# A two-block transformer on one core: eight modulation tiles and the value bias on VectorE, start-up loads and modulation reordered

## What is computed

```
def modulate(h, shift, scale):
    return h * (1.0 + scale[:, None, :]) + shift[:, None, :]
...
        ada_x = jnp.split(s_lat @ w_ada[l] + b_ada[l], 6, axis=-1)
        ada_c = jnp.split(s_ctx @ w_ada[l] + b_ada[l], 6, axis=-1)
        hc = modulate(rmsnorm(ctx, norm_mix_g[l]), ada_c[0], ada_c[1])
        pc = hc @ w_in[l][:, ML_START:MERGE_START] + b_in[l][ML_START:MERGE_START]
        _, ctx_state = mlstm_branch(pc[..., :ML_COLS], pc[..., ML_COLS:], ...)
        hx = modulate(rmsnorm(x, norm_mix_g[l]), ada_x[0], ada_x[1])
        yx, _ = token_mixer(hx, *mix_params, rows, GRID_W, ctx_state)
        x = x + ada_x[2][:, None, :] * yx
        hx2 = modulate(rmsnorm(x, norm_ffn_g[l]), ada_x[3], ada_x[4])
        x = x + ada_x[5][:, None, :] * expert_choice_ffn(hx2, w_router[l], ...)
```

## Time and profile before

| what | value |
|---|---|
| median of 3 runs | 2276.83 us (2274.57 to 2279.39) |
| the profiled execution | 2277.35 us, of which the span of the trace is 2275.5 us |
| PE busy | 1904.8 us (84%) |
| VectorE busy | 708.1 us (31%) |
| ScalarE busy | 335.3 us (15%) |
| mean granted TensorE clock | 0.923 |
| DMA | 648.59 MB |

### The profile page before, as it was taken

One profiled execution on the slowest core, in us unless ns is written; L12 is line 12 of the kernel. 1 busy time (PEld: TensorE's weight loads), 2 busy tenths in 40 slices (PEclk: granted clock), 3 DMA queues, 4 the chain that ended last, 5 costly groups with the idle time before them and its releaser, 6 DMA issues.

```text
span 2275.5 us, 30074 instructions
## 1 busy us (share of the span) xinstructions
PE 1904.8 (84%) x12730; PEld 1278.0 (56%) x12730; DVE 708.1 (31%) x1663; ACT 335.3 (15%) x759; POOL 0.2 (0%) x4
## 2 busy tenths in 40 slices
PE   7899999966666666666666679999999999999999
PEld 4688778521111111111111137868889978688899
DVE  3433334300000000000000025562556556625654
ACT  4132030200000000000000010260210012612100
POOL 0000000000000000000000000000000000000000
PEclk7999999987788888878788889999999999999999
DMA  7456578999999999999999995524644554246441
GB/s 265 167 186 215 192 248 308 398 429 428 428 429 429 428 429 428 429 429 429 429 429 429 429 401 181 183 77 167 241 149 166 187 204 166 94 167 227 162 167 56
DMA packets 147882, 648.59 MB, mean 285 GB/s; under 512 B 10645, under 2 KB 17410, under 8 KB 123016
## 3 DMA queue, kind: packets, MB, share of 16 engines
q1 hardware_dynamic: 144100, 643.81, 71.5%
q10 hardware_dynamic: 3684, 3.37, 0.5%
HBM read 646.10 MB, written 1.05 MB: 284 GB/s over the span
## 4 chain that ended last, share of the span: by engine, by line
PE 60%; DMA 33%; DVE 4%; issue 1%; ACT 1%; SPq 0%; ACTq 0%; DVEq 0%
DMA ring<-in_w_exp 33%; PE bank L2016 15%; PE bank L890 13%; PE bank L2699 6%; PE bank L1799 4%; PE bank L1551 4%; PE bank L2614 2%; PE bank L1814 2%; PE bank L904 1%; PE bank L933 1%; PE bank L931 1%; PE bank L611 1%; PE bank L768 1%; PE bank L1476 1%; PE bank L451 1%
## 5 line engine op out<-in xcount | busy, mean ns | idle before, releaser
L1799 PE MATMUL bank<-ring,arena 128*32 128x512 f32 x1968 | 301.1, 745 | 212.3 <-DMA ring<-in_w_exp 202.0
L1799 PEld LDWEIGHTS bank<-ring,arena 128*32 128x32 f32 x1968 | 60.2, 123 | 436.5 <-DMA ring<-in_w_exp 320.4
L890 PE MATMUL bank<-hx,ring 128*128 128x256 f32 x1344 | 293.2, 379 | 0.7 <-ACT hx L786 0.7
L890 PEld LDWEIGHTS bank<-hx,ring 128*128 128x128 f32 x1344 | 254.6, 190 | 37.5 <-issue 3.4
L1814 PE MATMUL bank<-ring,arena 128*32 128x512 f32 x1008 | 165.5, 799 | 77.5 <-DMA ring<-in_w_exp 66.6
L1857 DVE COPY arena<-bank 128x256 f32<-128x256 f32 x16 | 6.8, 424 | 525.8 <-PE bank L1804 525.8
L2016 PE MATMUL bank<-arena 128*128 128x256 f32 x672 | 151.0, 379 | 0.3 <-DVE arena L2065 0.3
L1814 PEld LDWEIGHTS bank<-ring,arena 128*32 128x32 f32 x1008 | 33.3, 134 | 193.8 <-DMA ring<-in_w_exp 111.2
L2016 PEld LDWEIGHTS bank<-arena 128*128 128x128 f32 x672 | 127.0, 190 | 17.5 <-DVE arena L2065 0.6
L1864 DVE COPY arena<-bank 128x256 f32<-128x256 f32 x16 | 6.8, 424 | 346.1 <-PE bank L1688 346.1
L2016 PE MATMUL bank<-ring,hx 128*128 128x256 f32 x448 | 105.8, 379 | 0.0
(11 more groups left out here) (484 smaller groups left out, 2285.9 us busy)
## 6 DMA issues: line engine op xcount, KB each, us to landing
ring<-in_w_exp SPq DMA_DIRECT2D x186, 2048.0 KB, 16.3
ring<-in_w_ada SPq DMA_DIRECT2D x36, 2048.0 KB, 12.2
ring<-in_w_in SPq DMA_DIRECT2D x29, 2048.0 KB, 9.2
ring<-in_w_ffn_in SPq DMA_DIRECT2D x20, 2048.0 KB, 8.0
ring<-in_w_ffn_out SPq DMA_DIRECT2D x10, 2048.0 KB, 7.8
ring<-in_w_out SPq DMA_DIRECT2D x6, 2048.0 KB, 10.9
arena<-in_w_exp SPq DMA_DIRECT2D x4, 2048.0 KB, 19.2
ring<-in_w_up_nsa SPq DMA_DIRECT2D x2, 2048.0 KB, 8.4
```

What stands on the lines that cost most here:

```text
L890: ins = pe.matmul(b[:, o:o + n], w[:, k, j * P:(j + 1) * P], h[:, k, :], start=k == 0, stop=k == KD - 1)
L1799: ins = pe.matmul(banks[s][32 * j:32 * j + 32, :], e_xe[:, 2 * t + kk, :], w[:, kk, 512 * j:512 * j + 512], start=t + kk == 0, stop=t + kk ...
```

## The change

1. **Start.** The three loads of the first filter layer go from ScalarE's queue to the head of SP's, the identity the other way. The sums of squares of ctx go behind the second filter layer on ScalarE. On VectorE the mean and the scale of the norm go behind all eight tap products, and the sums of the taps behind these. `act_tables` goes ahead of the copies of the turned x and ctx. The five spectra of order 0 go from ahead of the tables to between the second and third modulation tile.
2. **Modulation.** VectorE modulates x, ScalarE ctx. `dve_wide_first` replaces four T and four S steps by the order S1, T1, S2, T2 ("sums 6"), S3, T3 ("sums 7"), S4, T4; PE waits for these names in turn. `dve_gate_pad` moves behind it.
3. **Value bias.** The six bias matmuls go; VectorE adds a broadcast bias row (five additions).
4. **Later tiles 0 to 7** are multiplied on VectorE: eight chained operations of 128x512 a tile (`dve_later_sum`), placed as the diff shows, and PE sums over partitions by four matmuls a tile. Four `pe_later` calls stand in `pe_project` and four in `pe_branches`; the one behind `pe_mlstm_num(pe, 3)` is gone. The stream order follows.

```diff
@@ stream @@
-    tiles("v", wide(w_in, ML0 + 1024, ML0 + 1536))
+    tiles_and_ada("v", wide(w_in, ML0 + 1024, ML0 + 1536))
...
-        (tiles_and_ada if t < 1 else tiles)(f"hy{t}", wide(w_in, 512 * t, 512 * t + 512))
-    tiles_and_ada("o", wide(w_in, ML0 + 1536, ML0 + 2048))
+        (tiles_and_ada if t != 1 else tiles)(f"hy{t}", wide(w_in, 512 * t, 512 * t + 512))
+    tiles("o", wide(w_in, ML0 + 1536, ML0 + 2048))
...
-    tiles_and_ada("", [])
@@ def dve_filter_taps(v) @@
-        v.wait_ge(*K.loaded("load_dft"))
...
+        dve_stats_mean(v)
+        dve_stats_scale(v)
+        DV.stage("filter")
+        v.wait_ge(*K.loaded("load_dft"))
+        for o in range(2):
+            for c in range(NC):
...
@@ def pe_ada @@
-            if t == 2:
-                pe_spectra(pe, 1, (0, 1))
+            if t in ADA_FILL:
+                pe_spectra(pe, *ADA_FILL[t])
+    ADA_FILL = {1: (0, range(5)), 2: (1, (0, 1))}
@@ def pe_later(pe) @@
+            if i < ON_DVE:
+                pe.wait_ge(*at(f"later summed{i}"))
+                for j in range(4):
+                    ins = pe.matmul(banks[6][32 * j:32 * j + 32, (i % 4) * P:(i % 4 + 1) * P], ones[:, 0:32],
+                                    later_acc[i % 2][:, j * P:(j + 1) * P], start=True, stop=True)
+                ins.then_inc(*PE.step(f"full later rows{g}", f"later read{i}"))
+                continue
+    ON_DVE = 8
+    def dve_later_sum(v, i, part):
+        w = tile(v, f"later{i}")
...
+        for k in (0, 1, 2, 3) if part == 0 else (4, 5, 6, 7):
+            c = cT[:, k, 0:1]
+            if k == 0:
+                v.tensor_scalar(acc, w[:, k, :], c, None, ALU.mult).then_inc(*DV.step())
+            else:
+                v.wait_ge(*DV.last())
+                v.scalar_tensor_tensor(acc, w[:, k, :], c, acc, ALU.mult, ALU.add).then_inc(*DV.step())
@@ def pe_seven_wide @@
-                if key == "v" and bias is not None:
-                    ins = pe.matmul(o, ones[0:1, 0:P], bvrow[:, 256 * bias:256 * bias + 256], start=False, stop=True,
-                                    skip_group_check=True)
...
-        pe.wait_ge(*at("S project"))
-        pe.wait_ge(*at(f"T4 {key}"))
+        pe.wait_ge(*at("sums 6" if key == "k" else f"T2 {key}"))
...
+        if key == "k":
+            pe.wait_ge(*at("sums 7"))
@@ def dve_seven_wide @@
+                with_bias(u.rearrange("p (c n) -> p c n", c=2), nh)
+                v.wait_ge(*DV.last())
                 v.tensor_tensor((vc, vx)[th][:, :, 2 * nh:2 * nh + 2, 0:P], f(b), f(u), ALU.add).then_inc(*DV.step(*names))
+        def with_bias(x, nh):
+            v.tensor_tensor(x, x, spread(bvrow[:, 256 * nh:256 * nh + 256], 1, 2), ALU.add).then_inc(*DV.step())
@@ def dve_project(v) @@
+        dve_wide_first(v)
+        dve_gate_pad(v)
...
-        dve_seven_wide(v, "v", lambda i: None)
+        dve_seven_wide(v, "v", lambda i: dve_later_sum(v, i // 2, i % 2))
         dve_conv(v, 1)
+        for i in (2, 3):
+            dve_later_sum(v, i, 0)
+            dve_later_sum(v, i, 1)
         dve_rows(v)
         dve_conv(v, 2)
+        for i in (4, 5):
...
         dve_conv(v, 3)
         dve_context(v)
+        for i in (6, 7):
...
         dve_conv(v, 4)
@@ def act_branches(act) @@
         act.wait_ge(*at("tokc"))
+        act_later(act, 2)
+        AC.stage("mlstm")
...
-        act_later(act, 2)
```

More of the change, by code:

```diff
@@ L575, in act_ada @@
             ada_cols.append(f"full {name} col{t}")
[L576 to L577 removed]
+            if t - 1 in ADA_FILL:
+                act_spectra(act, *ADA_FILL[t - 1])
                 AC.stage("ada")
@@ L616, in pe_later @@
         PE.cur = stage
+    ON_DVE = 8
+    later_acc = [arena[:, 14368 + 512 * i:14880 + 512 * i] for i in range(2)]
+    def dve_later_sum(v, i, part):
+        w = tile(v, f"later{i}")
+        acc = later_acc[i % 2]
+        if part == 0 and i > 1:
+            v.wait_ge(*at(f"later read{i - 2}"))
+        for k in (0, 1, 2, 3) if part == 0 else (4, 5, 6, 7):
[5 more added lines that the diff above has]
+                v.scalar_tensor_tensor(acc, w[:, k, :], c, acc, ALU.mult, ALU.add).then_inc(*DV.step())
+        if part:
+            book.where[f"later summed{i}"] = DV.now
+            book.where[f"used {where[f'later{i}']}"] = DV.now
     def pe_later_turn(pe, g):
@@ L625, in act_later @@
     def act_later(act, g):
-        act.wait_ge(*at("m3 v"))
+        act.wait_ge(*at("v sums"))
         if g:
@@ L717, in act_normed, with act_modulate_c, dve_modulate_x @@
                 *AC.step(f"{key} normed"))
-    def act_modulate_x(act):
+    def act_modulate_c(act):
         AC.stage("norm")
-        act.wait_ge(*at("gain mix0"))
+        act.wait_ge(*at("gain c"))
         for k in range(KD):
-            act.activation(hcx[:, k, N:2 * N], scrx[:, k, :], ACT.Identity, bias=adaX[0][:, k:k + 1],
-                           scale=gs[:, k:k + 1]).then_inc(*AC.step("hx done"))
-    def dve_modulate_c(v):
+            act.activation(hcx[:, k, 0:N], scrc[:, k, :], ACT.Identity, bias=adaC[:, k:k + 1],
+                           scale=gsC[:, k:k + 1]).then_inc(*AC.step("hc done"))
+    def dve_modulate_x(v):
         DV.stage("norm")
-        v.wait_ge(*at("turncn in3"))
+        v.wait_ge(*at("turnxn in3"))
         for k in range(KD):
-            v.tensor_scalar(hcx[:, k, 0:N], scrc[:, k, :], gsC[:, k:k + 1], adaC[:, k:k + 1], ALU.mult, ALU.add).then_inc(
-                *DV.step("hc done"))
+            v.tensor_scalar(hcx[:, k, N:2 * N], scrx[:, k, :], gs[:, k:k + 1], adaX[0][:, k:k + 1], ALU.mult, ALU.add).then_inc(
+                *DV.step("hx done"))
     def pe_turn_in(pe, key, src):
@@ L923, in pe_seven_wide, with product @@
         S1, S2, S3, S4 = wide_s
-        def product(name, b, h, x, first=False, bias=None):
+        def product(name, b, h, x, first=False):
             for j in range(2):
@@ L969, in dve_wide_t, with dve_wide_first @@
             v.tensor_tensor(T4, quarter(w, 1, 0), T2, ALU.subtract).then_inc(*DV.step(f"T4 {key}"))
-    def dve_wide_s(v):
+    def dve_wide_first(v):
         S1, S2, S3, S4 = wide_s
+        w = tile(v, "k0")
+        T1, T2, T3, T4 = wide_t["k"]
+        v.wait_ge(*DV.last())
         v.wait_ge(*at("hc done"))
-        v.wait_ge(*at("hx done"))
         v.tensor_tensor(S1, wide_part(1, 0), wide_part(1, 1), ALU.add).then_inc(*DV.step())
-        s1 = DV.last()
-        v.tensor_tensor(S3, wide_part(0, 0), wide_part(1, 0), ALU.subtract).then_inc(*DV.step())
-        v.wait_ge(*s1)
-        v.tensor_tensor(S2, S1, wide_part(0, 0), ALU.subtract).then_inc(*DV.step())
-        v.wait_ge(*DV.last())
-        v.tensor_tensor(S4, wide_part(0, 1), S2, ALU.subtract).then_inc(*DV.step("S project"))
+        v.tensor_tensor(T1, quarter(w, 0, 1), quarter(w, 0, 0), ALU.subtract).then_inc(*DV.step())
+        v.wait_ge(*DV.last())
+        v.tensor_tensor(S2, S1, wide_part(0, 0), ALU.subtract).then_inc(*DV.step())
+        s2 = DV.last()
+        v.tensor_tensor(T2, quarter(w, 1, 1), T1, ALU.subtract).then_inc(*DV.step("sums 6"))
+        t2 = DV.last()
+        v.tensor_tensor(S3, wide_part(0, 0), wide_part(1, 0), ALU.subtract).then_inc(*DV.step())
+        v.tensor_tensor(T3, quarter(w, 1, 1), quarter(w, 0, 1), ALU.subtract).then_inc(*DV.step("sums 7"))
+        v.wait_ge(*s2)
+        v.tensor_tensor(S4, wide_part(0, 1), S2, ALU.subtract).then_inc(*DV.step())
+        v.wait_ge(*t2)
+        v.tensor_tensor(T4, quarter(w, 1, 0), T2, ALU.subtract).then_inc(*DV.step("T4 k"))
     def dve_seven_wide(v, key, after):
@@ L1012, in dve_seven_wide @@
         put(0, 1, b3, wu2, f"free {key}r3", f"{key} sums")
+        if key == "v":
+            v.wait_ge(*at("v copied"))
+            for c in range(NC):
+                x = vc[:, c, 0:2, 0:P]
+                v.tensor_tensor(x, x, bvrow[:, 0:256].rearrange("p (h e) -> p h e", h=2), ALU.add).then_inc(
+                    *DV.step("v sums"))
     def pe_project(pe):
@@ L1219, in dve_project @@
         v.wait_ge(*at("columns"))
-        for i in range(4):
-            dve_wide_t(v, "k", i)
-        dve_wide_s(v)
+        dve_wide_first(v)
+        dve_gate_pad(v)
         v.wait_ge(*at("full spec14"))
@@ L2916, in _ @@
         pe_turn_in(pe, "turncn", cin)
-        pe_spectra(pe, 0, range(5))
         pe_tables(pe)
```

57 lines of the change are left out of this document (26 added, 31 removed).

## The result

| | median us (lowest to highest, runs) | profiled run, span us |
|---|---|---|
| before | 2277.22 (2274.05 to 2279.45, 20) | 2277.35, 2275.5 |
| after | 2282.89 (2281.56 to 2284.78, 20) | 2284.72, 2282.9 |

The ratio is 1.0029, with a 95% interval of 1.0023 to 1.0035: the change makes the kernel slower by 5.7 us, a quarter of a percent. The forecast was 2276.0 and "no change that can be measured".

The account below looks back on a forecast made before the run. PE bounds until 353 us, expert weight loads from 462 to 1400. Gains of 5.7 + 4.9 + 8.8 us shrink to 1.6 through waits, less 0.7 at the branches' end: 0.9 us, median 2276.0, range 2266 to 2284.

Parts of the forecast that it names:

- the bias: Value product v: six bias matmuls and their effect on the neighbours go from PE's path, 4.9 us won.
- the modulation and the sums: k's second product starts at 72.7 instead of 77.78 and the clock stays up; PE 5.7 us ahead at product 7.
- the wait of 3.5 us ahead of the turn: After the taps PE waits 3.5 us for last tap, mean, scale and norm before turning x.
- the fourth part's price: Between v's end and the Hyena matmuls: 8.8 us of PE calls saved, but load and VectorE waits leave 1.6 us overall.
- hy0 lands at 136.4 ... 0.5 us: Behind v: hy0's load, queued behind tiles 2 and 3, lands after PE wants it at 135.9; wait 0.5 us.
- wanted at 150.9: 1.9 us: hy1's load, behind tiles 4 and 5, lands at 152.8, so PE waits 1.9 us.
- seven chained operations of 0.69 ... with 0.03 between, 5.5 us: One later tile on VectorE: a tensor_scalar of 0.47 and seven chained operations, 5.5 us in all.
- the o linear loses 1.5: Behind the wait for tiles 6 and 7 the clock is at half, costing the o linear 1.5 us.
- The rival in which the sums run at the rate of tensor_scalar: Later tiles take 3.8 us each, both VectorE waits shrink by 3.4; time 2269; chance 0.14 for VectorE half in the way.
- The end of the branches: Without the call the turn starts 0.3 us earlier, PE idles 4.1 us, the clock likely halves; 0.7 us lost.
- The start: From the first filter loads to the last modulation turn (63.2 against 64.04): the reordering earns 0.9 us.
- the clock stays low: After the pause ahead of the turn the clock rises only after the spectra, at 53: 7.3 us lost, 2283.3; chance 0.19.

Follow-up runs that it names:

- the kernel with all tiles on PE: Changed kernel with its fourth part undone (later tiles' sums, calls and stream as before; start, modulation and bias stay changed): 2264.74 us, ratio 0.9947.
- the fourth part alone: Kernel before with only the sums of tiles 0 to 7 on VectorE, their new calls, places and stream: 2293.15 us, ratio 1.0065.
- half of the sums: Changed kernel with VectorE leaving out four of the eight blocks of each of tiles 4 to 7: 2274.24 us, ratio 0.9988.
- the kernel with the last call moved: Changed kernel with the last call of later tiles (14 and 15) behind the last numerator again: 2281.94 us, ratio 1.0024.
- six summed in VectorE's idle time: Changed kernel with only tiles 0 to 5 summed on VectorE, placed around its row work: 2257.35 us, ratio 0.9917.

## Why the prediction was wrong

**What held.** The bound and that a shift before the merge arrives at the end; the bias (4.9 forecast; alone 4.9 in the trace and 4.7 by the medians); the modulation and the sums (with the start 5.7 forecast at product 7; 4.5 in the profiled pair, 5.7 in the kernel with all tiles on PE, where it begins at 80.49; the three parts together bring 10.5 us at v's end in that kernel's trace, against 5.7 + 4.9); the place and the size of the waits ahead of the state (6.4 and 6.40) and ahead of the call for tiles 6 and 7 (5 and 5.40); the wait of 3.5 us ahead of the turn; that a call fewer at the end of the branches only leaves PE idle.

**What failed: the fourth part's price.** By the prediction it costs, between v's end and the Hyena matmuls, 9.1 us (102.9 from 118.5 to 221.4, against 93.84). Measured: 15.0 in after and 15.6 where it was alone (129.06 to 238.49, less 93.84). Of the 5.9 us between forecast and after, 5.7 are these terms of the sum:
- "hy0 lands at 136.4 ... 0.5 us" and "wanted at 150.9: 1.9 us": 1.46 and 3.06, so 2.1 more. The order in the queue of loads was followed rightly, but counted from v's end hy0 was there 0.9 us and hy1 2.2 us later than reckoned.
- A term that wasn't there: the clock behind the load wait. It was counted for pauses of 5 us only. hy1 lost 1.4 in after, 1.7 in the kernel with the fourth part alone, and 3.0 with half of the sums, against its 14.08 elsewhere. So 1.4 more.
- "seven chained operations of 0.69 ... with 0.03 between, 5.5 us": 0.752 each, 0.79 from start to start, 6.0 us a tile. Tiles 4 and 5 are 1.0 of this (it shows as the wait of 1.06 ahead of tile 5's read), and from kw to the read of tile 7 it takes 11.95 us (197.18 to 209.13) instead of 11.0: 2.0 more for the four tiles.
- "the o linear loses 1.5": it lost 2.2. From the read of tile 7 to its end it takes 16.7 us instead of 16.3, and ScalarE behind it 2.9 instead of 3.1: 0.2 more.

The 0.69 came from an operation of the same name and width whose scalar is an immediate (L1412, after L1467). Here it is a column in SBUF, a value per partition. That this is the reason the other widths in the trace of after show (line, operation, form, count, busy us, mean ns of one); L840 has a column, L424 and L1467 an immediate, and all read and write SBUF:

```profile
L840 DVE SCALAR_TENSOR_TENSOR scr<-xT,small,rs 128x256 f32<-128x256 f32 x32 | 13.0, 479 | 0.1
L424 DVE SCALAR_TENSOR_TENSOR arena<-mg,arena 64x256 f32<-64x256 f32 x6 | 2.5, 418 | 0.2
L1467 DVE SCALAR_TENSOR_TENSOR arena<-arena 128x512 f32<-128x512 f32 x4 | 2.8, 692 | 10.7 <-ACT arena L1447 10.7
```

With a column it is 752 against 692 at 512 columns, 479 against 418 at 256, and 348 (L2831) against 285 (L2211) at 128: 60 to 63 ns more at each width. The trace of before had such rows too: the convolution (L1107), which the prediction used for its 4.4 us, takes 476 ns for 252 columns. The rival in which the sums run at the rate of tensor_scalar is refuted by the rows of the tiles: the first operation of each takes 0.48, the other seven don't. The table of the Trainium skill, page "VectorE: DVE Perf Modes", section "The perf-mode tier table", doesn't list the operation; 752 ns here against 481 for tensor_scalar at the same width agree with the reading that it has no double rate.

**The end of the branches** was priced at 0.7; from L1531 to the merge after takes 1.2 more than before, and the three other kernels without that call take 130.7 to 131.1 us. But with the call it takes 129.4 to 130.8 in nine traces, so a part of the 1.2 may be the clock of that one execution. With v's end at 119.9 instead of 118.5 this makes the whole miss at the merge: 5.9 + 0.5 + 1.4 = 7.8 us, against 7.9 from -0.9 to 7.0.

**The start** was forecast at +0.9. It is 1.8 when done alone, within the error of nothing, and -0.2 in the two profiled runs. In that of after the taps began at 16.52 instead of 16.1 and the turn took 6.53 us instead of the forecast 5.9. In the nine traces with the pause the turn took between 5.30 and 6.53, by how soon its transposes came to full speed. Of the rival "the clock stays low", nothing was found: it is at 1.00 from 40 us to the end of v.

**The sign** turned on a difference of two large sums, 19.4 us won and 18.5 given away, and the second held only the waits that I had found. The error of 5.9 us on it was larger than the result. A forecast of "same" at 0.57, with a rival slower by 5 us or more only through the clock at the start, left out the plainest one: that the waits and the sums are each a little longer than reckoned, and that a shorter pause too can be followed by the lower clock. The measured 2282.89 lies within the stated 2266 to 2284, but by luck: the upper part of that range was given to a clock that stays low at the start, and it did not.

## What to carry to other kernels

Moving work from the bound engine to an idle one pays only where the idle time lies in front of what the bound engine waits for. Eight tiles, four of them summed where PE waits for them, cost 16 to 18 us; six summed in VectorE's idle time won some 7. So read the idle engine's timeline against the deliveries between the two, and give a wait that the work itself brings (a later load, an eviction behind it) its own term. Price an operation by a row with the same kind of operands (here a column as the scalar), and a chained one by start-to-start distance. Give the low clock a price behind every pause of the sizes seen here, 2 to 6 us, as a chance and not only behind the longest.

## What the runs showed of the hardware

- **What the clock costs behind a pause varies from execution to execution.** A pause of about 3 us ahead of hy1 cost 1.4 us (after), 1.7 (the fourth part alone, 15.77 instead of 14.08), 3.0 (half of the sums, 17.12) and nothing in the kernel with the last call moved: there the same wait of 2.78 was followed by a linear of 14.08. The merge takes 29.55 or 27.86 us in traces of kernels with the same code there: 29.55 in before and 27.86 in the kernel with the last call moved, each behind a pause of 2.10 and the same rows ahead of it. The Trainium skill, page "TensorE: Matmul & The Clock Gate", section "HAM oscillation — how this bites in real kernels", lets each burst behind a pause pay again; these traces agree, except that not every one paid. The profiled run of after, 2284.72 us, is the second longest of its twenty, so the 7.4 us between the two traces hold 1.8 that the medians don't; that these are the clock's is likely and not shown.
- **The granted clock of a row is not the whole truth.** In the trace with all tiles on PE it reads 1.00 from 17 to 31 us, yet the taps take 13.99 us, as in before, where it reads 0.50. The length of matmuls of a known form decides.
- **scalar_tensor_tensor with a column as its scalar** takes 752 ns for 128x512, fifty-six times within 750 to 754, and with an immediate 692; the 60 ns are the same at 256 and 128 columns.
- **A chain of VectorE and ScalarE over 4 partitions** (the row work) takes 13.4 to 14.4 us from its first to its last VectorE instruction in six traces, with three table loads of 1.28 us on ScalarE, and it holds the eviction of the next linear. What VectorE does ahead of it delays PE by way of ScalarE when the chain starts late enough: PE waited 1.58 to 2.19 us in the three kernels where it starts 25.1 to 25.7 us behind v's end, and not where it starts 19.8 or 19.9 behind.
